# Two Scalar instructions change places in the stick-breaking attention units of a decoder layer

## The reference, cut to what matters

```
z = einsum('bthd,bshd->bhts', q[:, q0:kend], k[:, :kend]) * scale      # blocks of 128 queries
log_beta = log_sigmoid(z)
log_1m   = where(strict, log_sigmoid(-z), 0.0)
after    = cumsum(log_1m, axis=3, reverse=True) - log_1m
w        = where(strict, exp(log_beta + after), 0.0)                   # strict: s < t
out      = einsum('bhts,bshd->bthd', w, v[:, :kend])
```

## Time and profile before

| | |
|---|---|
| median of 3 runs | 1338.19 us (1337.03 to 1339.63) |
| time of the profiled execution | 1339.76 us |
| its span | 1338.0 us |
| PE busy | 1293.1 us, 97% |
| PE weight load busy | 1076.7 us, 80% |
| DVE busy | 806.6 us, 60% |
| ACT busy | 561.4 us, 42% |
| line 1992 (turning) in the chain that ended last | 1.9% |
| line 2005 (values) in that chain | 3.3% |
| line 1434 (scan) in that chain | about 1% |

### The profile page before, as it was taken

The page is one execution under the profiler, slowest core; times in us unless marked ns, Lnnn a source line. Parts: engine busy times, 40 slices in busy tenths (PEclk is TensorE's granted clock), DMA queues, the critical chain, the costliest instruction groups (busy, mean ns, idle before and its releaser), DMA issues.

```text
span 1338.0 us, 17189 instructions
## 1 busy us (share of the span) xinstructions
PE 1293.1 (97%) x6717; PEld 1076.7 (80%) x6717; DVE 806.6 (60%) x1094; ACT 561.4 (42%) x917; POOL 61.0 (5%) x69
## 2 busy tenths in 40 slices
PE   4999999998999999999999999999999999999998
PEld 2788878897888888888777888888888887887886
DVE  6643576687658888843788656565656533335333
ACT  4612212686547788831464333333333323222221
POOL 1101110130000001000000000000000000001001
PEclk9999999999999999999999999999999999999999
DMA  9343544100013325211323222212221164447443
GB/s 380 145 183 131 196 179 164 47 1 17 17 40 80 80 53 172 85 32 47 123 98 103 71 95 95 75 68 95 95 81 62 63 211 143 142 143 266 145 151 122
DMA packets 39389, 150.30 MB, mean 112 GB/s; under 512 B 4432, under 2 KB 4624, under 8 KB 37776
## 3 DMA queue, kind: packets, MB, share of 16 engines
q1 hardware_dynamic: 36976, 140.85, 31.0%
q0 software_dynamic: 2336, 8.39, 1.7%
HBM read 117.77 MB, written 24.12 MB: 106 GB/s over the span
## 4 chain that ended last, share of the span: by engine, by line
PE 87%; DVE 6%; ACT 3%; issue 2%; DMA 1%; POOL 0%; SPq 0%; DVEq 0%; ACTq 0%
PE ps L2233 28%; PE ps L1727 14%; PE ps L1716 10%; PE ps L1718 10%; PE ps L1717 10%; PE ps L2005 3%; PE ps L1992 2%; PE ps L1983 2%; PE ps L1950 1%; DVE left L1434 1%; PE ps L1951 1%; PE ps L1972 1%; DMA traw<-t_spill_d 1%; DVE beta L1439 1%; ACT omb L925 1%
## 5 line engine op out<-in xcount | busy, mean ns | idle before, releaser
L1716 PE MATMUL ps<-TH,dWH 128*128 128x512 f32 x352 | 137.1, 390 | 2.0 <-DVE dWL L1652 1.2
L1717 PE MATMUL ps<-TL,dWH 128*128 128x512 f32 x352 | 136.9, 389 | 0.0
L1718 PE MATMUL ps<-TH,dWL 128*128 128x512 f32 x352 | 136.9, 389 | 0.0
L2233 PE MATMUL ps<-h2H,slH 128*128 128x512 f32 x320 | 124.6, 389 | 0.0
L2233 PE MATMUL ps<-h2L,slH 128*128 128x512 f32 x320 | 124.5, 389 | 0.0
L2233 PE MATMUL ps<-h2H,slL 128*128 128x512 f32 x320 | 124.5, 389 | 0.0
L1650 DVE TENSOR_TENSOR TL<-traw,TH 128x512 fp32r<-128x512 f32 x44 | 30.5, 693 | 136.1 <-ACT TH L1058 136.1
L1038 ACT ACTIVATE slH<-ssum 128x512 fp32r<-128x512 f32 x80 | 50.4, 632 | 140.4 <-PE ps L2233 96.4
L1058 ACT ACTIVATE TH<-traw 128x512 fp32r<-128x512 f32 x44 | 27.8, 632 | 165.4 <-PE ps L1718 157.3
L1434 DVE TENSOR_TENSOR_SCAN left<-omb 128x255 f32<-128x255 f32 (+4 forms) x64 | 86.5, 1352 | 9.5 <-ACT omb L925 8.6
L1716 PEld LDWEIGHTS ps<-TH,dWH 128*128 128x128 f32 x352 | 66.1, 188 | 16.7 <-issue 1.5
(11 more groups left out here) (331 smaller groups left out, 3025.2 us busy)
## 6 DMA issues: line engine op xcount, KB each, us to landing
ada<-ada SPq DMA_DIRECT2D x12, 2048.0 KB, 9.4
draw<-down SPq DMA_DIRECT2D x44, 512.0 KB, 3.7
sraw<-gu SPq DMA_DIRECT2D x20, 1024.0 KB, 6.0
raw<-win SPq DMA_DIRECT2D x22, 512.0 KB, 4.5
traw<-t_spill_d SPq DMA_DIRECT2D x44, 256.0 KB, 3.9
t_spill_d<-tst SPq DMA_DIRECT2D x20, 512.0 KB, 3.0
x_in<-xT SPq DMA_DIRECT2D x4, 1024.0 KB, 8.6
qkl_spill_d<-qkl SPq DMA_DIRECT2D x8, 512.0 KB, 4.0
```

The lines of the kernel that those rows point to most:

```text
L1716: mm(out, lh, rh, start=first, stop=False)
L1717: mm(out, lh, rl, start=False, stop=False)
L1718: return mm(out, ll, rh, start=False, stop=last)
L2233: last = mm(ps[:, Q_BANK[q], :], l[q][:, w], r[:, c, :], start=(c == 0 and k == 0 and q not in (Q_G2, Q_S4)), stop=(c == 3 and k == 2), sk ...
```

## The change

In `stick_step` the second sigmoid of unit u, with its wait, now stands ahead of the copy of unit u-2 (and, in the first two units, ahead of the last two copies of the softmax attention). Nothing is added or taken away; the semaphores and what each instruction waits for stay as they are.

```
             A(omb[v % 2][:, 0:n], pair(2 * (v % 2), n), ACT.Sigmoid, scale=-(SBD ** -0.5)).then_inc(sem["s_nb"], 1)
             if u < 2:
                 mla_copy(NM - 2 + u, NU - 2 + u)
-            else:
+            act.wait_ge(sem["s_tr"], after(u - 2))
+            A(beta[v % 2][:, 0:n], pair(2 * (v % 2), n), ACT.Sigmoid, scale=SBD ** -0.5).then_inc(sem["s_b"], 1)
+            if u >= 2:
                 if u == 2:
                     act.wait_ge(sem["m_av"], after(NM - 1))
                 stick_copy(u - 2)
-            act.wait_ge(sem["s_tr"], after(u - 2))
-            A(beta[v % 2][:, 0:n], pair(2 * (v % 2), n), ACT.Sigmoid, scale=SBD ** -0.5).then_inc(sem["s_b"], 1)
             if u >= 4:
                 stick_output(u - 4)
```

## The result

| | before | after |
|---|---|---|
| median | 1338.91 us (1337.03 to 1342.65, 4 runs) | 1353.28 us (1352.52 to 1354.12, 4 runs) |
| ratio | | 1.0104, 95% interval 1.0086 to 1.0122 |
| span of the profiled execution | 1338.0 us | 1351.5 us |
| PE busy | 1293.1 us | 1294.0 us |

The forecast was 1351.5 us, from 1346 to 1356. PE does the same work; the time is nearly all waiting.

What follows compares the result with a forecast made beforehand. PE, busy 97% of the span, was taken as the bound. Six heads at 1.99 us make 11.9, less 0.3 is 11.6; plus 1.7 for the last head is 13.3, giving 1351.5 us on the median, range 1346 to 1356.

Steps and rivals of the forecast that it cites:

- two parts in each head: Chain of waits: from the 8-block scores through ACT and DVE, 4.73 us; then on PE to the next 8-block scores.
- The four turnings: PE's turnings of the 2, 4, 6 and 1-block units wait for later copies: 0.54 + 0.37 + 0.52 + 0.56 = 1.99 us per head.
- what the 8-block turning gives back: PE's 0.36 us idle before the 8-block turning, waiting for an undelayed multiplication, is taken back from 0.90, leaving 0.54.
- the heads with extra work: In heads carrying the other group's squares, the second sigmoid came late for the scores; this 0.3 us or so goes.
- The last head: Last head and the piece before it: turnings later, score waits of 0.22 and 0.58 gone; together 1.7 us, from 0 to 3.5.
- (a): PE waits for the copy only in part: 0.54 shrinks, two other terms come; 7 us in all, 1345; chance 0.08.
- (b): Faster: the earlier second sigmoid ends PE's waits, 6.8 us, 1331.4; with the copy's delay hidden, 1337; chance 0.03.
- (c): Delays add up: late scans in heads with squares or scaling; another 1 us in six heads, 1358; chance 0.04.
- (d): PE's granted clock falls from 2.4 to 1.2 GHz for one head: +17.6 us, 1369; chance 0.02.
- The Scalar price: What a moved sigmoid occupies on ACT, by start distances: 0.90, 0.37, 0.58, 0.80 us for 8, 3, 5, 7 blocks.

Runs made afterwards that it cites:

- experiments 1 to 4: The swap only in odd units, even units, the 8-block unit, or the 3, 5 and 7-block units, against the kernel before: 1.0096, 1.0001, 1.0043, 1.0082.
- experiment 8: The kernel before with the swap only in two units of the last head, its first and fourth: 0.9998, 1338.47 us.
- experiment 10: The kernel before with 8-block scores one step earlier, 7-block swap, two last-head swaps, and squares and scalings spread to where ACT waits: 0.9976, 1336.65 us.
- experiments 3 and 11: Against the kernel before: the swap in the 8-block unit alone, 1.0043; squares and scalings spread plus two last-head swaps, without earlier scores or 7-block swap, 0.9998.

## Why the prediction was right, point by point

**What bounds the stage.** PE, with two parts in each head. It held: the multiplication's wait disappeared when the copy's took its time (`1.40` and no wait at the 8-block turning), as the 0.36 was forecast to be given back.

**The four turnings.** The places were right, in the seven heads all four and no other, and experiments 1 to 4 show it by parts. The sizes: 2-block 0.90 forecast, 0.92 measured; 4-block 0.37, 0.33; 6-block 0.52, 0.54; 1-block 0.56, 0.59. The term that was mis-sized is what the 8-block turning gives back: 0.36 forecast, 0.53 measured. The 0.36 was the idle time in the trace. In the changed kernel this transposition need not wait and starts 0.17 us before the modelled end of the mask matmul ahead of it:

```profile
441.32 0.23 PE L1953 MATMUL ps<-mask_sb,identb 128*128 128x128 bf16 x1
```

That end is 441.55 and the turning starts at 441.38, so a wait here moves the next start by the idle time shown and this overlap. A head lost 1.88 and not 1.99; six heads 10.9 and not 11.6. The 0.3 us that was to go in the heads with extra work did go: before they took 18.63, after 20.34, and the others 20.32 to 20.34.

**The last head.** 1.7 us forecast, 1.1 measured from the seventh 8-block unit on. The forecast added the single terms roughly; experiment 8 shows one of them: of the 0.8 us that the scores' waits were to give back, 0.15 came, and the rest went into a wait for the multiplication.

**The rivals.** (a) failed at the 2-block turning, which came 0.92 late in full. (b) was right in its direction for two units and wrong by its size. (c) did not occur: the heads with squares or scalings take 20.32 to 20.34 like the others. (d) was set aside because the clock had been 1.00 with short waits. For the changed kernel that held: its profile has the clock at 1.00 in all seven heads, and the mean was 0.995 to 0.998 in its four runs. But this was in part luck, by what the other kernels show. With the same 1.4 us wait, which the forecast itself named, the kernel with the odd units had a fall in one head of seven and the one with three buffers in three, at 1.6 us each; seven of them would have been 11 us. In the stage falls came more often behind a longer single wait. The Trainium skill, page "TensorE: Matmul & The Clock Gate", section "A second HAM failure mode: psum-queue depth-cycling", warns of frequent short idle times; the stage with 28 waits for the copy of up to 0.5 us (3, 5 and 7-block units) stayed at 1.00 here, and the one with a single wait of 2.4 us per head did not.

**The Scalar price.** By the trace's distances the four turnings were to be late by 0.90, 0.37, 0.52 and 0.56 us, 2.35 in all, before anything is given back; measured are 2.38. The page "ScalarE: Activation LUTs" of the Trainium skill, section "What ACT_TABLE_LOAD costs", makes it 2.53 as an estimate with the same slack, so the trace's distances were nearer.

**The sum.** 13.3 forecast, 12.0 in the profile's stage, 14.4 between the medians. The forecast was 1.3 us too high in the stage. That 1351.5 came out below the measured 1353.28 all the same has two sources that lie outside the change: 1.5 us at the start of the profiled execution, whose time is the median, and the 1.6 us by which the forecast went down from the profiled execution of the kernel before to the median of its three runs. With its fourth run that median is 0.85 us below the profiled execution, so that the 14.4 between the medians are 12.0, 1.5 and 0.85. A fit to all runs of all kernels, with a level for each kernel and one slope of time against mean clock, gives 0.88 us per 0.001, and at equal clock the change costs 13.2 us (plus or minus 1.1). The same fit gives the kernel of experiment 10 a gain of 2.0 us (plus or minus 0.7).

## What to carry to other kernels

Between two instructions that one event releases on the same engine, the first place belongs to the one for which the bounding engine waits; the price of giving it away is the other's distance to the next start, less the slack of the waiter, unit by unit. An order that is wrong in one place can pay in another once the work that it frees is moved to cover what it delays: the same swap cost 14 us everywhere, and in one unit of eight it was part of a version whose stage is 1.4 us shorter. Units of unequal size want the question asked for each of them.

## What the runs showed of the hardware

Five kernels here have one PE wait of 1.25 to 1.42 us in each of seven heads, at the 2-block turning. PE's granted clock fell to 0.50 behind 7 of these 35 waits: in no head of the changed kernel, in one with the odd units swapped, one with the extra sigmoid, two with the 8-block unit alone, three with three buffers. Each such fall cost 1.6 us. Behind waits of 2.3 to 2.5 us it fell in six heads of seven, and a fall cost 1.7 or 3.1 us. Why it falls behind one wait and not behind the next of the same length stays open.

The single wait does not explain every fall. In the profiles of experiments 3 and 11 the clock was at 0.50 for some 11 us, from 309 to 320 and from 308 to 319 us, ahead of the stage and in work that no kernel here changes (one window in experiment 11's kernel and in the kernel before, the granted clock behind POOL's number):

```profile
310.00:318.00 8.00, 7.04 (x24) 5.60 (x24) 2.49 (x4) 3.13 (x10) 0.94 (x1) 0.50 0.00 0
310.00:318.00 8.00, 7.04 (x46) 5.67 (x46) 4.08 (x8) 4.23 (x13) 0.94 (x1) 1.00 0.02 4
```

The longest wait shortly before it, 0.78 us, stands in the kernel before as well, where the clock stayed at 1.00. From that wait to the first 8-block sigmoid the two profiles with the fall take 4.2 us more (111.5 against 107.3). Differences of a few us between runs of one kernel can come from there, which is why the sizes above are read from the heads and not from the medians.
